# Moving the operand-sum jobs of GpSimd and the order of VectorE's splits in a chunked gated MLP block

## The reference, cut to what matters

```python
h = rmsnorm(x, norm_mix_g)
z = gelu(h @ w_in); u, v = split(z, 2)              # 1024 features each
v = rmsnorm(v, v_g)
s = einsum('gts,bnsgc->bntgc', tril(w_s), v) + b_s  # within chunks of 128 tokens
x = x + (u * s) @ w_out
a = relu(rmsnorm(x, norm_mlp_g) @ w1)
out = rmsnorm(x + (a * a) @ w2, final_g)
```

## Time and profile before

| what | value |
|---|---|
| three runs, lowest, median, highest | 1849.44, 1854.7, 1864.49 us |
| the profiled execution: its own time, its span | 1849.99 us, 1847.7 us |
| PE busy | 1784.2 us, 97% of the span |
| DVE busy | 1138.0 us, 62% |
| ACT busy | 786.1 us, 43% |
| POOL busy | 445.4 us, 24% |
| DMA over the span | 244 GB/s |

### The profile page before, as it was taken

The page is one execution under the profiler, slowest core; times in us unless marked ns, Lnnn a source line. Parts: engine busy times, 40 slices in busy tenths (PEclk is TensorE's granted clock), DMA queues, the critical chain, the costliest instruction groups (busy, mean ns, idle before and its releaser), DMA issues.

```text
span 1847.7 us, 20069 instructions
## 1 busy us (share of the span) xinstructions
PE 1784.2 (97%) x8036; PEld 1481.4 (80%) x8036; DVE 1138.0 (62%) x1136; ACT 786.1 (43%) x862; POOL 445.4 (24%) x418
## 2 busy tenths in 40 slices
PE   9999299999899999999999999999999999999998
PEld 8788188888688888888878888888888888888886
DVE  3561487456288665665576665676567666866665
ACT  5822325462423744443463434454433335333333
POOL 2443542443442123330001311110234101000002
PEclk9999599999999999999999999999999999999999
DMA  9556375765566788886867777699977645854552
GB/s 362 218 190 231 136 272 205 274 250 183 205 228 248 292 271 269 279 288 216 302 234 252 255 256 250 222 401 319 309 281 279 248 182 188 299 196 182 187 206 108
DMA packets 135452, 451.68 MB, mean 244 GB/s; under 512 B 8128, under 2 KB 9152, under 8 KB 119616
## 3 DMA queue, kind: packets, MB, share of 16 engines
q1 hardware_dynamic: 101344, 323.77, 49.5%
q0 software_dynamic: 27344, 101.19, 15.3%
q10 hardware_dynamic: 6672, 25.44, 3.7%
HBM read 320.35 MB, written 130.02 MB: 244 GB/s over the span
## 4 chain that ended last, share of the span: by engine, by line
PE 79%; DMA 10%; POOL 6%; ACT 3%; issue 2%; DVE 1%; ACTq 0%; DVEq 0%; POOLq 0%
PE bank L1448 64%; PE bank L1409 8%; PE bank L1260 4%; DMA job<-in_mlp_w 2%; DMA job<-xs 2%; DMA w1sum<-job 1%; PE bank L1249 1%; DMA job<-in_a_w_out 1%; DMA w_raw<-in_a_w_in 1%; ACT junk L653 1%; DMA wosum<-job 1%; DMA xs<-job 1%; POOL x_rstd L495 1%; PE bank L1282 1%; POOL job L529 1%
## 5 line engine op out<-in xcount | busy, mean ns | idle before, releaser
L1448 PE MATMUL bank<-x_hi,u_hi 128*128 128x512 f32 x896 | 349.1, 390 | 1.2 <-DVE c L1158 1.2
L1448 PE MATMUL bank<-x_hi,u_lo 128*128 128x512 f32 x896 | 348.6, 389 | 0.0
L1448 PE MATMUL bank<-x_lo,u_hi 128*128 128x512 f32 x896 | 348.6, 389 | 0.0
L1448 PE MATMUL bank<-d_lo,a_hi 128*128 128x512 f32 x896 | 348.5, 389 | 0.0
L1448 PE MATMUL bank<-d_hi,a_hi 128*128 128x512 f32 x896 | 348.5, 389 | 0.0
L1448 PE MATMUL bank<-d_hi,a_lo 128*128 128x512 f32 x896 | 348.5, 389 | 0.0
L1158 DVE TENSOR_TENSOR Y<-bank,Y 128x512 f32<-128x512 f32 x208 | 137.9, 685 | 179.1 <-PE bank L1448 178.7
L925 DVE TENSOR_TENSOR u_lo<-u_raw,u_hi 128x1024 fp32r<-128x1024 f32 x112 | 149.0, 1331 | 147.7 <-ACT u_hi L610 147.4
L615 ACT ACTIVATE d_hi<-d_raw 128x2048 fp32r<-128x2048 f32 x56 | 107.4, 1918 | 288.5 <-DMA d_raw<-w2sum 161.0
L919 DVE TENSOR_TENSOR w_lo<-w_raw,w_hi 128x2048 fp32r<-128x2048 f32 x45 | 108.2, 2411 | 150.3 <-ACT w_hi L605 150.3
L1448 PEld LDWEIGHTS bank<-x_hi,u_hi 128*128 128x128 f32 x896 | 168.2, 188 | 36.5 <-DVE u_lo L925 1.9
(11 more groups left out here) (125 smaller groups left out, 2791.9 us busy)
## 6 DMA issues: line engine op xcount, KB each, us to landing
a_raw<-a2s SPq DMA_DIRECT2D x56, 1024.0 KB, 7.8
a2s<-sums SPq DMA_DIRECT2D x32, 1280.0 KB, 8.1
job<-in_mlp_w POOLq DMA_DIRECT2D x32, 1024.0 KB, 7.0
u_raw<-w1sum SPq DMA_DIRECT2D x64, 512.0 KB, 4.7
d_raw<-w2sum SPq DMA_DIRECT2D x32, 1024.0 KB, 4.9
w_raw<-in_a_w_in SPq DMA_DIRECT2D x31, 1024.0 KB, 5.9
u_raw<-in_mlp_w SPq DMA_DIRECT2D x48, 512.0 KB, 5.3
d_raw<-in_mlp_w SPq DMA_DIRECT2D x24, 1024.0 KB, 5.3
```

The costliest lines, as they stand in the source:

```text
L1448: ins = pe.matmul(bank_of(g, j)[:, :], stationary[x_part][:, k, j * P:(j + 1) * P], moving[y_part][:, k, :], start=i in (0, 1, 3) and k == ...
```

## The change

POOL's jobs are placed anew. Before the rstd of v in blocks 0 to 3 there were 1, 2, 2 and 2 jobs and now there is 1 in each; behind it there were 5, 4, 4 and 4 and now 2, 6, 2 and 7. So the blocks hold 21 jobs in place of 24. In the cycles there were two jobs in cycles 0 and 1, none in 6, 7 and 8, one in each other; now two in cycles 0 to 3 and one in each of 4 to 15. Three jobs in place of five are left for the down-projection.

DVE's order in a block: `scale_u(q, 0)` moves ahead of `split_w(w + 8)`. In blocks 0 and 2 the eight instructions of `split_h(q + 1)` stood in one piece behind `gates(q, 2)`; now four stand ahead of `gates(q, 2)` and four behind `gates(q, 4)`. PE's wait for `hT_ready` at the start of a block is cut in two, one for each half.

```diff
             for q in range(BLOCKS):
-                next_jobs(2 if q else 1)
+                next_jobs(1)
                 rstd(v_sq, v_squares(q), v_ms, v_ms_done, v_rstd, v_rstd_done, q)
...
-                next_jobs(4 if q else 5)
+                next_jobs((2, 6, 2, 7)[q])
                 if q % 2:
...
             for u in range(UP):
                 pool.wait_ge(products, step_done(u * STEPS))
-                if not UP // PAIRS - 2 <= u <= UP // PAIRS:
-                    next_jobs(2 if u < 2 else 1)
+                next_jobs(2 if u in (0, 1, 2, 3) else 1)
...
                 split_w(w + 7)
+                scale_u(q, 0)
                 split_w(w + 8)
-                scale_u(q, 0)
                 gates(q, 0)
                 split_w(w + 9)
                 if q % 2:
                     split_o(q // 2, 0)
+                else:
+                    split_h(q + 1, range(KU))
                 gates(q, 2)
-                if q % 2 == 0:
-                    split_h(q + 1, range(KD))
                 scale_u(q, 1)
                 gates(q, 4)
                 if q % 2 == 0:
+                    split_h(q + 1, range(KU, KD))
                     gates(q, 6)
...
                 if q:
-                    pe.wait_ge(hT_ready, q * KD + KD)
+                    pe.wait_ge(hT_ready, q * KD + KU)
...
                 token_major(hT[q], w, bank_set(q, 0), 0, first_v)
+                if q:
+                    pe.wait_ge(hT_ready, q * KD + KD)
```

## The result

| | median us | lowest to highest | runs |
|---|---|---|---|
| before | 1854.3 | 1848.93 to 1864.49 | 6 |
| changed | 1843.1 | 1841.49 to 1843.69 | 6 |

The ratio is 0.9937, with a 95% interval of 0.9909 to 0.9965. The change makes the kernel faster by 0.6%. I had forecast 1812 us with a range of 1794 to 1832, so the time lies 31 us over the forecast and 11 over the range. The profiled execution took 1843.32 us, its span 1841.5 (before: 1849.99 and 1847.7).

The account below looks back on a forecast made before the run. PE, busy 1784.2 of 1847.7 us, was taken as the bound, idle mostly in 47.1 us of waits for scale_u. Forecast: 1850.0 - 52.8 - 1.6 - 3.2 + 13.9 + 1 + 5 = 1812.3 us, range 1794 to 1832.

Parts of the forecast that it names:

- both stalls at L1313: PE's waits in blocks 1 and 3 for scale_u, 37.0 and 10.1 us; with the clock, 52.8 us gained.
- the exchange: Cycles 6, 7 and 8, now with a job each: +5 us, bounds 0 and 15.
- rival A: POOL keeps pace behind block 3, no cycle 0 stall: 1798 us, or 1793 with exchange jobs hidden; chance 0.27.
- rival D: v_rstd early but PE still waits at L1313, for products or w_lo: a few us, inside the range; no separate chance.
- behind v_rstd, block 3: seven jobs: Seven jobs take 136.7 us, so x1_rstd is 10.5 us late and PE stalls at cycle 0: +13.9 us with clock.
- rival C: Slower than before: x1_rstd 48 us late behind seven jobs of 25.6 us each; with all else over 1836, 0.07.
- Block 1's six jobs, taken as nothing: Block 1, behind v_rstd: six jobs at 16 to 20 us fit before x1_rstd is needed; cost nothing.
- ACT isn't held: Block 3's late x1_rstd: DVE's split_u(2) and split_x(0, 2) wait behind it and PE for them, but not ACT.
- the same lateness seen from another side: SP's wait for job 19's store before loading x sums, some 8 us late: no separate cost.
- DVE's order and the cut of hT: scale_u ahead of split_w in block 0, -1.6 us; split_h cut in two, blocks 0 and 2, -3.2 us.
- Contention in cycle 0: A w1 job beside the splits of cycle 0 slows DVE: +1 us, bounds 0 and 4.4.
- the port rule of the Trainium skill: Cycles 0, 7, 8: two-SBUF-input DVE and SBUF-reading POOL instructions block each other; about 1 us more in all, not used.

Follow-up runs that it names:

- balanced kernel: Changed kernel with jobs 1, 1, 2, 1 ahead of v norms and 2, 5, 3, 5 behind: 1797.02 us; without jobs in cycles 6 to 8, 1790.49 us.
- the last experiment: Against the kernel with six jobs behind block 3's norm, the four x jobs moved ahead of two w1 jobs: 1819.85 us.
- the kernel with six jobs: Changed kernel with six jobs in place of seven behind block 3's v norm, job 20 going to cycle 0: 1829.68 us.

## Why the prediction was wrong

**The direction and the mechanism held.** POOL's early v norm took away both stalls at L1313 whole, and with them the stretches at a low clock. The balanced kernel shows the gains whole where jobs don't eat them: 1790.5 us with no jobs at the exchange, against 1793 for rival A with a hidden exchange. POOL waits for v's squares in blocks 1 and 3 (34.6 us in block 3), and rival D didn't come.

**The step that failed is the size of the term "behind v_rstd, block 3: seven jobs".** It put x1_rstd at the end of 136.7 us of jobs, 10.5 us late and 13.9 with the clock; the jobs took 160.5 us, and the stall was 33.0 and 2.9. The rates were taken from rows that don't stand for those places:

- *The first four jobs* end at 531.63, 91.9 us from the start. I gave three of them the quiet rate of the four x jobs ahead of the norm, 18.7 each, and the fourth the busy one: 3 x 18.7 + 20.2 = 76.3 us. But what stood behind the norm wasn't quiet: they take 20.7, 21.4, 27.2 and 22.5 us, with a store of 12.06 us in the third, and additions of up to 3.23 us, against 1.29 alone, in the other three. What slowed those additions and that store was not tried. The four jobs that stood in that stretch of the program before, 497.30 to 577.87, came with 10 us of idle PE among them and still took 21.4 each with their stores. The rows for this stretch were there, and I used them for the other half.
- *The last three jobs* take 68.0 us to the issue of the last store at 599.60, against 3 x 20.15 = 60.4. They lie behind the last job whose rate I had. By PE's place in the program the job stored at 577.87 before is the one stored at 526.71 now. The fifth job's load meets the first loads of cycle 0 (SyncE issues two x_raw and four u_raw from 532.1 to 541.3; 10.78 us of wait), the sixth a 2 MB store of x1, the seventh the five loads of x. Before, all of these came when POOL had nothing left to do but wait for squares. The slack of 25.87 us was no measure of what fitted in, since the transfers of that stretch had never shared it with a job. That these transfers set the rate is shown by experiment only for the five loads of x (the last experiment); for the fifth and sixth job it is read from their times.

The rival C had this as its mechanism, and the rate from which it decides, 25.6 us a job counting the last store, was sound: by that count, with 5 us for the store, 23.5 were measured, between my 20.2 and it. My bound of 21.4 for all seven was the highest mean of four jobs that I had, and it was no bound for a stretch that those rows don't cover.

**Block 1's six jobs, taken as nothing,** cost 8.8 us by the trace and 9 by experiment. The prediction itself said that 20 us each was "at the edge" and then gave the edge no price; the same rate error, 22.3 for 16 to 20, decides it.

**"ACT isn't held" was wrong, and "the same lateness seen from another side" too.** The store of job 19 and the loads behind it are a path of their own, 12.7 us of waits once the first path is short. In the changed kernel it cost nothing by itself, but ACT's x_hi waited 12.75 us there, and by the last experiment the burst of loads that it releases lengthens the job whose load falls among them (16.08 us of wait in place of 8.57).

**The small terms:** the exchange was +5, measured +9.0 in the trace of the changed kernel (5.7 of waits, 3.3 of clock, which the term left out) and 6.5 by experiment in the balanced kernel, where the clock holds. DVE's order and the cut of hT were -4.8, measured -6.0 in the trace and -6.4 and -5.7 by experiment; the term left out the fall of the clock at the start of block 1. Contention in cycle 0 has no wait. Its price was read from two different instructions, a multiplication of 0.69 us (L1168) and another operation of 1.78 (L1171); the reading holds all the same, since L1171 took 0.68 us in the kernel before at 890.01, where POOL adds nothing. By the port rule of the Trainium skill (SBUF — State Buffer, "Who interferes with whom") the prediction's estimate for these terms would have been about 1 us more. The runs here do not tell that from none.

**The range** failed since only 7 in 100 were kept for more than 1836 us, and since the terms of x1_rstd in blocks 1 and 3 and the rate that they share were varied as if only one of them could be off. With 22.5 us for every job the prediction's own working gives seven jobs of 157 us, 31 late in block 3 in place of 10.5, and some 11 late in block 1: with the clock of both, 1812.3 + 20.5 + 11 + 2 = about 1846 us.

## What to carry to other kernels

When work in a queue is moved, its rate has to be read from the stretch to which it goes, by what the DMA engines and DVE do there, not from the stretch that it leaves; behind the last row that was measured there is no bound, and waiting time of the queue isn't free time of the transfers. Behind a small result that others wait for, count how many jobs fit before the next such result at the rate of that stretch: here five fitted with 3.7 us to spare, six cost 4.6 to 10 us at that wait, seven 33. And an edit that saves PE time ahead of a wait whose end another engine's queue sets is worth nothing until that wait is gone (here it even cost 0.3%), so its value is measured only in the kernel that has both.

## What the runs showed of the hardware

- A 1 MB load by POOL's queue landed in 7.0 us at the median before, and 17.9 us after its issue where seven loads of SyncE's queue and a 2 MB store of ACT's were under way (354 GB/s at a DMA share of 0.93, from 575 to 594 us). At the exchange two such loads waited 12.68 and 12.51 us.
- What the clock costs behind a wait shows no clear dependence on the length of the wait. In the 8 us from the end of a PE wait of 6.70 us the mean granted clock is 0.76, after 10.02 us 0.77, after 32.96 us 0.68, after 32.72 us 0.66; in the kernel with six jobs it is 0.65 after 6.57 us, in the one with x first 0.82 after 6.77, and in the kernel before 0.71 after 36.97 and 0.58 after 10.17. So each return cost 1.4 to 3.4 us. The 16 transposes that come first took 3.1 to 3.7 us then, 1.91 at the full level.
- A wait of 2 to 3 us can cost as much again in clock, or nothing. In the 6 us from the end of the waits at the exchange the clock is 0.72 after 1.90 us, 0.74 after 2.65 and 1.00 after 2.35 in the changed kernel, 0.51 after 2.96 in its repeat, and 1.00 after 2.11 and 3.15 in the balanced kernel. What decides between the two was not tried.
